# Three landing buffers ahead of a six-slot weight ring, filled early and copied in by ScalarE; the last expert block written out apart

## The reference

```python
mod = silu(c) @ ada_w + ada_b                      # six rows of 1024: shifts, scales, gates
h = rmsnorm(x, norm_mix_g) * (1 + sc1) + sh1
x = x + gt1 * hybrid_mixer(h, ...)                 # causal pooling || gated DeltaNet, 8 heads
h = rmsnorm(x, norm_ffn_g) * (1 + sc2) + sh2
x = x + gt2 * moe_ffn(h, ...)
out = rmsnorm(x, final_norm_g)

def moe_ffn(h, ...):                               # top 4 of 32 experts
    logits = h @ router_w + router_b
    top_val, top_idx = top_k(logits, 4); comb = softmax(top_val)
    for each expert e, for its tokens:
        hu = x_b @ w1[e] + b1[e]                   # 1024 -> 2048
        glu, lin = min(hu[0::2], 7), clip(hu[1::2], -7, 7)
        act = glu * sigmoid(1.702 * glu) * (lin + 1)
        y = act @ w2[e] + b2[e]                    # 1024 -> 1024
    out = sum over a token's experts of comb * y
```

## Time and profile before

| | us |
|---|---|
| median of 3 runs | 1385.56 |
| lowest and highest of them | 1385.40, 1387.38 |
| the profiled execution, whole | 1386.72 |
| its span in the trace | 1384.9 |
| PE busy | 1288.4 (93%) |
| DVE busy | 392.9 (28%) |
| ACT busy | 184.7 (13%) |
| granted TensorE clock, mean over the span | 0.984 |

### The profile page before, as it was taken

How to read it: one execution, slowest core, us unless ns; L and a number is a source line. 1 busy time by engine, 2 the same in 40 slices (tenths; PEclk the granted TensorE clock), 3 DMA queues, 4 the chain that set the end, 5 groups by cost and what they waited for, 6 DMA issues and landing times.

```text
span 1384.9 us, 17303 instructions
## 1 busy us (share of the span) xinstructions
PE 1288.4 (93%) x6461; PEld 621.9 (45%) x6462; DVE 392.9 (28%) x987; ACT 184.7 (13%) x394; POOL 56.9 (4%) x51
## 2 busy tenths in 40 slices
PE   4999989999999999999899999999999999999996
PEld 1888868889843333333233332333333332333322
DVE  1698446642243112111121111121121111121112
ACT  2000113322121001100001000010011000010002
POOL 0210004321000000000000000000000000000000
PEclk8999999999998999999999999999999999999999
DMA  9997550006445999999999999699999999999994
GB/s 375 370 331 274 182 183 1 1 1 246 156 164 224 425 425 427 427 427 426 425 425 428 428 425 428 252 429 425 425 426 429 425 428 426 424 427 428 425 428 201
DMA packets 65493, 471.60 MB, mean 341 GB/s; under 512 B 3981, under 2 KB 4298, under 8 KB 31674
## 3 DMA queue, kind: packets, MB, share of 16 engines
q1 hardware_dynamic: 64672, 469.61, 82.2%
q10 hardware_dynamic: 538, 1.13, 0.2%
q0 software_dynamic: 256, 0.48, 0.2%
HBM read 470.16 MB, written 1.05 MB: 340 GB/s over the span
## 4 chain that ended last, share of the span: by engine, by line
PE 51%; DMA 42%; DVE 3%; SPq 2%; issue 1%; ACT 1%; POOL 0%; DVEq 0%
DMA ring<-in_exp_w_dram 41%; PE bank L1219 17%; PE bank L771 13%; PE bank L1245 6%; PE bank L1119 2%; PE bank L1190 2%; DMA ring<-in_w_in_dram 2%; PE bank L1257 1%; SPq L481 1%; PE bank L1211 1%; PE bank L926 1%; PE bank L1041 1%; PE bank L1025 1%; PE bank L1038 1%; PE bank L816 0%
## 5 line engine op out<-in xcount | busy, mean ns | idle before, releaser
L1219 PE MATMUL bank<-ring,work 128*64 128x512 f32 x2112 | 472.3, 598 | 49.0 <-DMA ring<-in_exp_w_dram 49.0
L1219 PEld LDWEIGHTS bank<-ring,work 128*64 128x64 f32 x2112 | 144.9, 137 | 373.6 <-issue 273.7
L1245 PE MATMUL bank<-ring,work 128*64 128x512 f32 x1056 | 233.9, 595 | 0.0
L771 PE MATMUL bank<-region_h,ring 128*128 128x256 f32 x704 | 158.0, 386 | 2.3 <-DVE region_h L1373 1.2
L771 PEld LDWEIGHTS bank<-region_h,ring 128*128 128x128 f32 x704 | 135.3, 194 | 21.3 <-DMA ring<-in_w_in_dram 2.8
L1245 PEld LDWEIGHTS bank<-ring,work 128*64 128x64 f32 x1056 | 73.0, 137 | 137.3 <-issue 137.3
L728 ACT ACTIVATE work<-work 128x256 f32<-128x256 f32 x66 | 27.6, 418 | 766.3 <-DVE work L1710 766.3
L1710 DVE TENSOR_SCALAR work<-bank 128x256 f32<-128x256 f32 x66 | 27.6, 419 | 347.7 <-PE bank L1219 347.7
L1737 DVE TENSOR_TENSOR work<-bank,work 128x512 f32<-128x512 f32 x33 | 22.8, 692 | 315.6 <-PE bank L1245 315.6
L1190 PE MATMUL bank<-qkv,work 128*64 128x512 f32 x272 | 65.9, 606 | 0.6 <-DVE work L1650 0.6
L1257 PE MATMUL bank<-work 64*128 64x512 f32 x264 | 65.6, 615 | 0.8 <-DVE work L1737 0.8
(11 more groups left out here) (295 smaller groups left out, 897.3 us busy)
## 6 DMA issues: line engine op xcount, KB each, us to landing
ring<-in_exp_w_dram SPq DMA_DIRECT2D x192, 2048.0 KB, 23.7
ring<-in_w_in_dram SPq DMA_DIRECT2D x13, 2048.0 KB, 13.5
ring<-in_ada_w_dram SPq DMA_DIRECT2D x12, 2048.0 KB, 13.8
ring<-in_w_gdn_out_dram SPq DMA_DIRECT2D x2, 2048.0 KB, 10.0
ring<-in_w_out_dram SPq DMA_DIRECT2D x2, 2048.0 KB, 15.3
ring<-in_w_pool_out_dram SPq DMA_DIRECT2D x1, 2048.0 KB, 7.9
region_x<-in_x_dram SPq DMA_DIRECT2D x2, 512.0 KB, 4.0
region_x<-in_x_dram ACTq DMA_DIRECT2D x2, 512.0 KB, 5.2
```

What stands on the lines that cost most here:

```text
L771: mm = nc.tensor.matmul(out_ap, w(k) if w else w_slot(n, j, k), rhs[:, k, :], start=(k == 0), stop=(k == kc - 1))
L1219: mm = nc.tensor.matmul(bank[b][h * SLOTS:(h + 1) * SLOTS, :], xT[:, c % 4, c // 4, :], slot_as(q, 2)[:, i, lo:lo + 512], start=False, sto ...
L1245: mm = nc.tensor.matmul(bank[2][o * SLOTS:(o + 1) * SLOTS, :], actT[:, b, c, h, :], slot_as(4 + b, 2)[:, h, lo:lo + 512], start=(b + h + c ...
```

## The change

What it does:

- **Memory.** `work`, the ring and a ninth area become one tensor `arena` of nine pieces of 2 MiB. Pieces 0 and 1 are the mixer's `work`, pieces 2 to 7 the ring, piece 8 holds small front-only things (`spare`) and `region_h`. Once the mixer is done, pieces 0, 1 and 8 are the three landing buffers `landing[0..2]`. The temporaries of the expert blocks move into `region_y`, `region_z` and `qkv`; four constant tables used in the front alone move into `spare`.
- **Loads.** Expert 0 goes into the ring as before. Chunks 0 and 1 of expert 1 are loaded into `landing[0]` and `landing[1]` between chunks 1 and 2 of expert 0, and chunk 2 of expert 1 into `landing[2]` once the routing scores are done. From then on chunks 0, 1, 2 of every expert go to a landing buffer (`load_staged`) and chunks 3, 4, 5 straight into the ring (`load_direct`). `load_staged(e, j)` waits until ACT has made the copy of chunk `j` for the last block of expert `e - 1`.
- **Order of the loads.** For loop values 1 to 7: (e+1, 0), (e+1, 1), (e, 3), (e+1, 2), (e, 4), (e, 5). For 8 to 30: (e, 3), (e, 4), (e, 5), (e+1, 0), (e+1, 1), (e+1, 2). Then 3, 4, 5 of expert 31.
- **Copies.** `stage(n, j, e)` on ACT copies a landing buffer into ring slot `j` for block `n`, two instructions of 128x2048 each. Three stages for block n+1 stand at the end of ACT's block n; those of chunks 0 and 1 for block 1 stand at the start of block 0. A second block of the same expert copies the same buffers again.
- **Last block.** Written out apart: PE reads chunks 0 to 2 from the landing buffers, there is no gather and turn for a next block, `combine` of the block before stands between chunks 1 and 2, and chunks 3 and 5 of expert 31 are loaded in halves with a semaphore each.
- **The end.** A square root on a scratch value stands ahead of the squares (it brings the table in); the root takes half of the sum of squares as its bias; the output goes out in four pieces of 256 KiB. `fin_g` is loaded at the end into the ring.
- **Small.** Four semaphores are merged into others; b1, b2 are loaded earlier; DVE makes four more 1-row instructions ahead of `vec_route` (counts less 2, as float and as integer); a memset moves behind the addition to `h2`.

The core of the diff:

```diff
-        ring = sb("ring", [P, RING, KC, CW])
+        arena = sb("arena", [P, (RING + STAGED) * SLOT])
+        work = arena[:, 0:2 * SLOT]
+        ring = arena[:, 2 * SLOT:8 * SLOT].rearrange("p (r c n) -> p r c n", r=RING, c=KC)
+        landing = [arena[:, i * SLOT:(i + 1) * SLOT].rearrange("p (c n) -> p c n", c=2) for i in (0, 1, 8)]
...
-            stream(0, 0)
-            sp.wait_ge(vec_x1, 4)
...
-            with sp.Fori(1, E) as e:
-                stream(e, first_block_of(sp, e))
-            for t in range(T):
-                sp.wait_ge(vec_out, t + 1)
-                sp.dma_start(out[0, t * P:(t + 1) * P, :], fin[:, t, :]).then_inc(out_done, 16)
+            def load_staged(e, j):
+                sp.wait_ge(act_staged, 3 * copied_blocks_of(sp, e - 1) + (j + 1))
+                load(e, j, landing[j])
+            def load_direct(e, j):
+                sp.wait_ge(used[j], USES + first_block_of(sp, e))
+                load(e, j, slot_as(j, 2))
+            for j in range(2):
+                sp.wait_ge(used[j], USES)
+                load(0, j, slot_as(j, 2))
+            sp.wait_ge(pe_o, 6)
+            sp.wait_ge(vec_ossq, 4)
+            for j in range(2):
+                load(1, j, landing[j])
...
+            sp.wait_ge(vec_x1, 4)
+            sp.wait_ge(pe_logits, 2)
+            load(1, 2, landing[2])
+            sp.wait_ge(vec_route, 1)
+            with sp.Fori(1, AHEAD) as e:
+                load_staged(e + 1, 0)
+                load_staged(e + 1, 1)
+                load_direct(e, 3)
+                load_staged(e + 1, 2)
+                load_direct(e, 4)
+                load_direct(e, 5)
+            with sp.Fori(AHEAD, E - 1) as e:
+                for j in range(3, 6):
+                    load_direct(e, j)
+                for j in range(3):
+                    load_staged(e + 1, j)
...
-            def serve(n):
+            def serve(n, last=False):
+                first = isinstance(n, int)
+                if not last:
+                    e_next = expert_of(act, n + 1)
+                if first:
+                    stage(n + 1, 0, e_next)
+                    stage(n + 1, 1, e_next)
                 for b in range(2):
...
                 turned_act(n, 1)
+                if not last:
+                    for j in range(2 if first else 0, 3):
+                        stage(n + 1, j, e_next)
+            def stage(n, j, e):
+                act.wait_ge(landed[j], 16 * (e + USES + 1))
+                act.wait_ge(used[j], USES + n)
+                for i in range(2):
+                    ins = nc.scalar.activation(slot_as(j, 2)[:, i, :], landing[j][:, i, :], ACT.Copy)
+                ins.then_inc(act_staged, 1)
...
-                for q in range(4):
-                    w1_chunk(n, q, e)
+                for q in range(3):
+                    pe.wait_ge(act_staged, 3 * n + (q - 2))
+                    w1_chunk(q, slot_as(q, 2))
+                pe.wait_ge(landed[3], 16 * (e + USES + 1))
+                w1_chunk(3, slot_as(3, 2))
                 gather(n + 1)
                 combine(n - 1)
                 finish_block(n, e)
+            def serve_last(n):
+                e = E - 1
+                bias(n)
+                for q in range(2):
+                    pe.wait_ge(landed[q], 16 * (e + USES + 1))
+                    w1_chunk(q, landing[q])
+                combine(n - 1)
+                for q in (2, 3):
+                    pe.wait_ge(landed[q], 16 * (e + USES + 1))
+                    w1_chunk(q, slot_as(q, 2) if q == 3 else landing[q], last=True)
+                finish_block(n, e, last=True)
```

More of the change, by code:

```diff
@@ new lines, in program @@
+        sel = early[:, 384:512].rearrange("p (t s) -> p t s", t=T)
+        each4 = early[:, 512:768].rearrange("p (t r e) -> p t r e", t=T, r=TOPK)
+        wsel = early[:, 768:1024].rearrange("p (t a s) -> p t a s", t=T, a=2)
+        gatew_twice = late[:, 0:256].rearrange("p (t n) -> p t n", t=T)
+        gatewT = late[:, 256:512]
+        wselT = late[:, 512:768]
+        blocks_row = late[0:E, 768:896]
+        upto = late[:, 896:928]
+        ends = late[:, 928:960]
+        block_cols = late[:, 960:964]
@@ L732, in serve, with fin_square @@
                 turned_act(n, 0)
-                turned_x(n + 1)
+                if not last:
+                    turned_x(n + 1)
                 turned_act(n, 1)
+                if not last:
+                    for j in range(2 if first else 0, 3):
[6 more added lines that the diff above has]
+                ins.then_inc(act_staged, 1)
             gathered(0)
             turned_x(0)
+            act.wait_ge(vec_route, 1)
             serve(0)
-            further_blocks(act, serve)
-            for i in range(4):
+            serve(further_blocks(act, serve), last=True)
+            nc.scalar.activation(stat[:, 1, 2:3], small[:, 16:17], ACT.Sqrt)
+            def fin_square(i):
                 act.wait_ge(vec_fin, i + 1)
@@ L1241, in w2_chunk @@
                 for h in range(2):
+                    if last and b and h:
+                        pe.wait_ge(last_in, 16)
                     for c in range(2):
@@ L1319, in _ @@
             finish_block(0)
-            count = further_blocks(pe, serve)
-            combine(count - 1, last=True)
+            n_last = further_blocks(pe, serve)
+            serve_last(n_last)
+            combine(n_last, last=True)
         @block.vector
@@ L1728, in serve @@
                 dve.wait_ge(pe_gather, n + 1)
-                select(e_next, start_next)
+                if not last:
+                    select(e_next, start_next)
                 dve.wait_ge(pe_hu, n + 1)
@@ L1733, in serve @@
                 gated(n, 1)
[L1734 to L1735 removed]
+                if not last:
+                    dve.wait_ge(pe_gather, n + 2)
+                    mark(e_next)
                 dve.wait_ge(used[5], n + USES + 1)
```

313 lines of the change are left out of this document (170 added, 143 removed).

## The result

The changed kernel takes 1388.89 us (median of 20 runs, 1384.2 to 1391.05), the kernel before 1385.99 (20 runs, 1382.88 to 1390.99). The ratio is 1.0021, 95% interval 1.0013 to 1.0029: slower by 2.9 us. The sign was forecast and the time lies in the range, but the forecast said +7.1, more than twice what was lost. The profiled execution took 1388.31 us with a span of 1386.4; the one before 1386.72 with 1384.9.

The account below looks back on a forecast made before the run. Landings at the transfer rate were taken to bound the kernel, PE having 2.7 us to spare per block. Terms 1.5 + 6.6 + 1.3 + 0.2 - 2.5 = +7.1 us on 1385.56 gave 1392.7 us, range 1380 to 1398.

Parts of the forecast that it names:

- first restart: Start of the stream and its second wait on an ACT copy, transfers running again from 480.3 us: +1.5 us.
- early loop: Loop values 1 to 7: closed chain of 30.84 us against 29.52 of transfers, five holes of 1.3 us: +6.6 us.
- two-block expert: Expert 15: transfer holes of 14.6 us together, split in three, where one of 13.3 was: +1.3 us.
- last block: Last expert block: PE ends 7.9 us behind the last byte instead of 7.7: +0.2 us.
- tail: After the last w2 matmul: table load hidden, scaling by pieces, stores of half the size: -2.5 us.
- K: Copy of one chunk by ACT, with the hand-over: 3.8 us, bounds 3.3 and 5.1.
- I: Hand-over from the release of a slot to transfers running: 1.1 us.
- L: Hand-over from the last byte of a chunk to PE's start on it: 1.95 us.
- T: Time at which the last byte lands; in the last block PE was to end 7.9 us after it.
- Contention: Slower rival: ACT's copies slow the stream of transfers, 1% on 183 chunks being 9 us: 1401 us; chance 0.09.
- No change: Rival: the early loop's chain is not longer than the transfers, so its 6.6 us go: 1386.1 us; chance 0.14.
- Faster: Rival: landing buffers bridge the expert with two blocks and early holes vanish: 1380.0 us, possibly 1370; chance 0.17.

Follow-up runs that it names:

- Kernel 1: Changed kernel with AHEAD = 2 instead of 8, so from expert 2 on chunks 3, 4, 5 load ahead of the next expert's 0, 1, 2: 1378.87 us, ratio 0.9965.
- kernel 2: Changed kernel with AHEAD = 14 instead of 8, keeping the interleaved load order for six more experts: 1396.57 us, ratio 1.0093.
- kernel 3: Changed kernel with a third ACT instruction (128x512) added to each copy before its buffer is released: 1399.73 us, ratio 1.0108.
- kernel 7: Changed kernel, same load order, with each copy shared: ACT copies the first half of a chunk, VectorE the second: 1384.02 us, ratio 0.9988.
- Kernel 6: Changed kernel with AHEAD = 2 and, in the last block, the previous block's `combine` moved behind chunk 3: 1376.2 us, ratio 0.993.
- kernel 4: Kernel before with the new end alone (table load ahead of the squares, root with bias, four stores instead of two): 1382.26 us, ratio 0.9988.
- kernel 10: Changed kernel with AHEAD = 2, the late `combine`, and chunk 2 of expert 1 loaded after the routing instead of before: 1376.76 us, ratio 0.9933.
- the changed kernel's second profile: Profile from a rerun of the changed kernel without any edit: 1389.07 us, ratio 1.002.

## Why the forecast was right in direction and wrong in size

To compare terms across two executions I measure from PE's first w1 matmul of block 0 (before 426.25, after 424.50) and compare places with equally many chunks still to come. Between the two executions, span less anchor grows from 958.65 to 961.9, that is +3.25; up to the anchor the changed kernel was 1.75 faster, hence +1.5 of span. These two profiles have the same clock at the start of block 0 and at chunk 3 of expert 2. The last block's term is what the others leave of the sum.

| term | forecast | measured | from |
|---|---|---|---|
| first restart | +1.5 | -0.2 | chunk 3 of expert 2, 494.49 |
| early loop | +6.6 | +3.2 | expert 15, 870.37 |
| two-block expert | +1.3 | +1.65 | 868.42 to 1000.92 |
| last block | +0.2 | +1.9 | last w2 ends 1375.71 |
| tail | -2.5 | -3.3 | 14.0 to 10.7 |
| sum | +7.1 | +3.25 | |

**The mechanism was right, and sizes of its terms were off both ways.** The forecast's sum is 3.85 us too high. The early loop was set 3.4 and the first restart 1.7 too high, the last block 1.7 too low, and that last miss hid part of the first two: that no more was missed is partly luck. The hole of ten microseconds at 470, the waits of SP on ACT's copies, the closed chain of the early loop, the split hole at the two-block expert and the old rate behind expert 10 are all in the profile, and kernels 1, 2, 3 and 7 change the time in the way it says. Kernel 1, with the same early loads, is 7.5 us ahead of the kernel before at expert 15 where the changed kernel was 3.0 behind; so the early loads brought something which this order gave away, though no kernel was run without any of them.

**The early loop was mis-sized, and this is the main error.** The step was the length of the chain: 9.23 to the end of the turn, K 3.8, I 1.1, three chunks 14.76 and L 1.95, together 30.84 us. The trace has, for expert 2 to 3, 503.59 - 494.49 = 9.10 to the start of the copies, 3.71 for the pair (ending at 507.30), and 524.76 - 507.30 = 17.46 for I, three chunks and L. So I + L is 2.70, not 3.05. Together 30.27; the next periods are 30.2, 30.1 and 30.1. Of the 0.57 us too many, 0.13 are the turn of the activations, 0.09 the copy and 0.35 the two hand-overs, which had been read from window shares, as if every busy share were full rate. Read from bytes they look different one by one as well: the copy that releases (3, 0) ends at 476.95 and transfers start at about 478.8, so I is some 1.8 us where the step had 1.1, and L some 0.9 where it had 1.95. Where a hole is a small difference of two large numbers (30.8 less 29.5), an error of 2% in the one halves the hole, and the five passes multiplied it. Some 0.6 us per pass, not 1.3, is what the trace shows.

The price of the copy came out well: 1.90 us for 128x2048 and 3.71 for the pair, where I took 3.8. The Trainium skill (ScalarE: Activation LUTs, section on what ACT_TABLE_LOAD costs) gave an estimate of 3.7, and the measurement agrees with it.

**The first restart.** The step was "against before that is 480.3 - 434.5 - (6 + 3) x 4.92", +1.5 us. What the changed kernel does was nearly met: the copy that releases (3, 0) ends at 473.24 + 3.71 = 476.95, which is 52.45 us behind the anchor for a forecast of 479.2 - 426.25 = 52.95 (0.5 less), and 17.54 us later PE starts chunk 3 for a forecast of 17.8 (0.3 less). The larger error is in the kernel before: its start of the stream, 434.5, was read from a share. The landing with as many chunks to come is the twelfth, forecast 8.25 + 12 x 4.92 + 1.95 = 69.2 behind the anchor; counted back from 870.33 in chunks of 4.92 it is 70.2 (0.9 more). 1.5 - 0.5 - 0.3 - 0.9 is -0.2: the second hole had used up the head start exactly.

**The two-block expert** was +1.65 for +1.3. Its windows in the changed kernel:

```profile
880.00:885.00 5.00, 5.00 (x30) 2.30 (x28) 0.00 (x0) 3.51 (x6) 0.00 (x0) 1.00 0.12 48
885.00:890.00 5.00, 5.00 (x30) 1.39 (x26) 0.60 (x1) 5.00 (x3) 0.00 (x0) 1.00 0.48 147
...
900.00:905.00 5.00, 5.00 (x26) 1.64 (x24) 2.08 (x6) 0.42 (x1) 0.00 (x0) 1.00 0.61 262
905.00:910.00 5.00, 5.00 (x30) 2.22 (x28) 1.41 (x4) 2.72 (x7) 0.00 (x0) 1.00 0.96 360
910.00:915.00 5.00, 5.00 (x26) 1.69 (x24) 0.00 (x0) 5.00 (x3) 0.00 (x0) 1.00 0.36 100
```

Three gaps in the transfers instead of one, as forecast. From 868.42 to 1000.92 are 132.5 us with four experts' transfers (118.1), a hole of 14.4; before, 870.33 to 1060.13 with six (177.1), a hole of 12.7.

**The last block** was the second error. The step said that PE "ends at T + 7.9 instead of 7.7"; it ended 9.5 behind it. (Chunk 2 of expert 30 starts at 1327.61, so by copy and the forecast's L its last byte came at 1321.95, and nine chunks later is 1366.2.) 1.2 us of the excess of 1.6 is the clock: I charged the w2 matmuls at 7.09 us and did not ask what PE did just before. Without a gather, and with the `combine` moved ahead, PE worked 0.44 of 2 us there. Kernel 6 has the same matmuls at 7.09 us with the `combine` in the gap. PE ends block 31 where the forecast has it (1346.59 is T - 19.6, which is 9.9 behind the last byte of expert 30). The last block's bias, w1 chunks and `combine` take 17.0 us for 16.8, and from the end of chunk 3 (1363.56) to the first w2 matmul (1367.46) it is 3.9 where the forecast's sum leaves 3.6. These 0.5 us are the rest.

**The tail** gave 3.3 instead of 2.5, and kernel 4 measures it alone at 3.0 in the profile, 2.8 by the medians and 1.7 by the ratio (0.1 to 3.2 by its interval, so the forecast's 2.5 is not excluded).

**The rivals.** Contention is refuted: periods of 29.53 beside ACT's copies, and 29.5 in kernel 3 with 15% more copying. The rule of the Trainium skill (SBUF — State Buffer, section on its two separate sides), that DMA and engines use different ports, agrees with these rows. "No change" was half true: the chain of the early loop was longer than the transfers, but by half of what I had, and the measured 1388.9 lies between its 1386.1 and the forecast. "Faster" did not happen with this order, and happens with another.

**What stays open.** The front took 1.75 us less in the profiled execution. Most of it is a stretch at about 128 us where PE's clock is at its lower level: 32 small matmuls take 5.4 us before and 3.9 in the changed kernel. The other profiles do not tie this to the change. Kernel 4 has the old layout and 5.33 us for these matmuls, and yet reaches its first w1 matmul at 424.66, as early as the changed kernel; of the ten profiles with the new layout nine have 3.7 to 3.9 us and kernel 10 has 5.12. So the 1.75 us may well be chance, and without them the spans differ by the 3.25 of the table, near the +2.9 of the medians. What decides between the two levels of the clock at this and the other places named here was not found.

## What to carry to other kernels

A queue that issues in order is only as early as its slowest-released entry: loads into a staging buffer, which wait for a copy, go behind the loads whose targets are already free, and a prefetch gained ahead of the loop is lost at the first such wait. Before an order is chosen, add up the closed chain (landing, use, copy, release, transfer) and set it against the period of the transfers; where they differ by a few per cent, take the hand-overs from the starts of instructions, not from the shares of windows. And near the end of a kernel, look at what TensorE does just before its last large group, for a gap there is often paid twice, as idle time and as a lower clock. And before a step of a microsecond or two in one profile is put down to an edit, look whether the same matmuls ran at the other clock.

## What the runs showed of the hardware

- A gap does not always lower TensorE's clock. Behind idle times of 5.51 and 2.97 us (kernel 3) and 3.17 us (the changed kernel's second profile) sixteen matmuls took 5.25 to 5.35 us, behind 3.15 (kernel 3) and 3.33 us (its first profile) 3.65. Behind the gap of 2.97 us, which ends at 529.68, the granted clock was still 1.00 up to 530 and 0.67 from 530 to 532. The length of one gap alone does not decide it, and the same place of the same program came out both ways.
- The same holds for the first sixteen w1 matmuls of block 0: 3.65 us in five of the twelve profiles, 5.3 in seven.
- In the last block, gaps of 1.1 and 1.4 us with two small matmuls between them were followed by the lower clock in six of seven profiles (8.25 and 8.78 us for 32 matmuls) and not in kernel 2 (7.09); where the gap was filled it was 7.09 three times out of three.
- ACT's 128x2048 fp32 copy takes 1.90 us, a pair 3.71; VectorE's copy of that size 1.23 us (kernel 7, mean of 96). Neither changes the period of the transfers beside it (29.5 us per expert in all of these kernels).
- In a window that holds the start of a stream, share and bytes disagree: 475 to 480 has a share of 0.38 but 105 GB/s, a quarter of the full rate. In the kernel before, the bytes of 434 to 440 us put the start at 435.1 where the share gave 434.5, and what follows speaks for a start that is later still.
